# Six of 64 modulation rows move from TensorE to VectorE, in the opening and in the last attention body

## The chip, the cores and the metric

The kernel runs on one core of a Trainium2 chip. The metric is the device time of one execution in microseconds; the median of the runs counts.

## The reference, cut to what matters

Two transformer blocks run one after the other on 256 tokens of width 2048, all in float32. The first one is modulated by a vector `c`:

```python
c_act = jax.nn.silu(c)
mod = c_act @ ada_w[l] + ada_b[l]                    # ada_w: 2048 x (6 * 2048)
sh1, sc1, g1, sh2, sc2, g2 = jnp.split(mod, N_MOD, axis=-1)
h = rms_norm(x, mix_pre_g[l]) * (1.0 + sc1) + sh1
y = hybrid_mixer(h, ...)      # proj = h @ w_in; attention over q, k, v; u = a * sigmoid(g),
                              # depthwise conv with 31 taps, layer_norm, silu; mix @ w_out
x = x + g1 * rms_norm(y, mix_post_g[l])
h = rms_norm(x, ffn_pre_g[l]) * (1.0 + sc2) + sh2
x = x + g2 * rms_norm(swiglu_ffn(h, ...), ffn_post_g[l])
```

The six parts of `mod` are parts 0 to 5. Parts 0 and 1 are made first, from a tensor of their own. Part 2 (`g1`) is wanted at the end of the first mixer, part 3 (`sh2`) and part 4 (`sc2`) after it, part 5 (`g2`) after the first feed-forward.

## The kernel before, in words

**Products.** Every weight arrives from HBM in halves: a half is 128 partitions x 1024 floats (512 KB), one slot of a ring of four (`RING`). SyncE issues the load once VectorE has finished with the slot, ScalarE rounds it (`w_hi`, line 580), VectorE makes the rest (`w_lo`, line 1173), and TensorE multiplies it with the rounded and the remaining part of the activations: 24 matmuls with 256 columns. ScalarE and VectorE work up to three halves ahead of TensorE (`LEAD`). A half that TensorE takes in the opening is recorded at lines 2078 to 2080, one of the attention bodies and of `w_out` at lines 2205 to 2207.

**Order of the stages around the change.** First the opening: eight column groups of `w_in` (those of `a` and `g`), whose last quarter is the loop `for g in range(OPEN)`. Then four bodies of twelve halves (q, k and v of two heads each), with the attention of the heads before between them (`attend1`), and the taps of the convolution on ScalarE and VectorE (`CONV_UNITS`, `CONV_OPS`, a count for each step). In the last body comes the layer norm of the convolution: its sums are products with `ones` at line 2244. Then `w_out` with 32 halves.

**The rows.** A row is 128 rows of `ada_w` for one part, 128 x 2048 floats (1 MB); each of parts 2 to 5 has 16. Row number `a` counts on from 0 (rows 0 to 15 are part 2, 16 to 31 part 3, 32 to 47 part 4). GpSimd issues the loads in order into a ring of three slots, `ADA_SLOT[a] = a % 3` up to row 47; a load waits until the row that was in its slot before has been used (`ada_load`, line 523). A row is used in one of two ways:

- On TensorE (`ada_row`, `ada_products`, line 2018): four matmuls with the row as the moving side, recorded as eight. These are the rows in `TIMED`.
- On VectorE (`early_row`, lines 1418 and 1420): `acc` is set to the row times its entry of `cact`, or has it added. These are the rows in `SUMMED`. `sum_rows` on TensorE (line 2215) then adds `acc` over the partitions to the bank in which TensorE has its own rows of the part.

Before, part 2 has all its 16 rows on TensorE: six in the opening (one ahead of each half from g = 2) and ten in body 0 (one ahead of each of the halves n = 0 to 9). Part 3 has twelve on TensorE (two each ahead of n = 0, 4 and 9 of bodies 1 and 2) and four on VectorE (n = 3 and 7). Of part 4, rows 32 to 35 are on TensorE in body 3 (n = 5, 7, 9, 11), rows 36 and 38 in `w_out`, and the other ten on VectorE in `w_out`. ScalarE copies the finished bank (`copy_rows`), and TensorE turns it into columns (`turn_rows`).

Every engine takes its instructions in order, and every wait is on a semaphore that another engine or a transfer raises.

Of the kernel before, what the change touches and what calls it, by code (L numbers as in the profile page):

```python
# [7 lines left out]
KT = D // 128  # L8
# [37 lines left out]
ADA_HEADS = (tuple(range(10)), (0, 0, 4, 4, 9, 9), (0, 0, 4, 4, 9, 9), (5, 7, 9, 11))  # L46
ADA_HEADS_ADDED = ((), (3, 7), (3, 7), ())
# [7 lines left out]
SUMMED = [a for a in range(4 * KT) if KT < a < 2 * KT and a % 8 in (2, 5) or a == 2 * KT + 5 or a >= 2 * KT + 7]  # L55
TIMED = [a for a in range(4 * KT) if a not in SUMMED]
SUMMED_3 = sum(a < 2 * KT for a in SUMMED)
# [95 lines left out]
def build(nc, tokens, params, conv_taps, f_bias, ada_first, ada_w, w_in, w_out, w_gate, w_up, w_down, w_in_2, w_f_2,  # L153
# [4 lines left out]
    with ctx:  # L158
# [411 lines left out]
        def _(act):  # L570
# [224 lines left out]
            def heads1(pair, last=False):  # L795

                body = 0 if pair is None else pair + 1
                for n in range(12):
                    convert()
                    if last and n == 11:  # L800
                        act.activation(warm[:, :], eps[:, 0:1], ACT.Silu)
                    if pair is None and n == 10:
                        act.wait_ge(ada_used, KT)
                        copy_rows(2, B_N)
                    if last and n == 1:
                        act.wait_ge(acc_summed, 1)
# [12 lines left out]
                    if last and n == 10:  # L819
                        root(SEQ, (ln_summed, 1), DA)  # L820
# [7 lines left out]
            for n in range(32):  # L828
# [13 lines left out]
                if n == 25:  # L842
                    act.wait_ge(acc_summed, 2)
# [320 lines left out]
        def _(dve):  # L1164
# [242 lines left out]
            def early_row(first=False):  # L1407
# [7 lines left out]
                if first:  # L1415
                    if summed:
                        dve.wait_ge(acc_summed, 1)
# [36 lines left out]
            taken = 0  # L1454
            for g in range(OPEN):
# [3 lines left out]
                convert()  # L1459
                conv_ops(g)  # L1460
# [54 lines left out]
            for body in range(4):  # L1515
                for n in range(12):
# [13 lines left out]
                    if n in ADA_HEADS_ADDED[body]:  # L1530
                        early_row(summed == 0)
# [21 lines left out]
            for n in range(32):  # L1553
# [12 lines left out]
                if n in ADA_ADDED:  # L1566
                    early_row(n == ADA_ADDED[0])
# [406 lines left out]
        def _(pe):  # L1974
# [40 lines left out]
            def ada_products(rows, slot, kt, b):  # L2015

                for g in range(4):
                    mm = pe.matmul(bank[32 * g:32 * g + 32, b, :], cact[:, kt:kt + 1].to_broadcast([128, 32]),  # L2018
                                   rows[:, slot, 512 * g:512 * g + 512], start=kt == 0, stop=kt == KT - 1 and b == B_N)
                return mm  # L2020

            def ada_row(n, b):
# [4 lines left out]
                ada_products(ada_raw, slot, ADA_ROW[a][1], b).then_inc(ada_used, 1)  # L2027
# [183 lines left out]
            def sum_rows(n):  # L2211

                pe.wait_ge(row_added, n)
                for g in range(4):
                    mm = pe.matmul(bank[32 * g:32 * g + 32, 3, :], ones[:, 0:32], acc[:, 512 * g:512 * g + 512],
# [3 lines left out]
            for body in range(4):  # L2219
                v_ready = used[2]  # L2220
                for n in range(12):
# [4 lines left out]
                    if body == 0 and n == 8:  # L2226
                        pe.wait_ge(ag_up, 4)
                    if body == 1 and n == 1:
                        turn_rows(2, B_N)
                    if body == 3 and n == 0:  # L2230
                        sum_rows(SUMMED_3)
# [17 lines left out]
            for n, (j, q) in enumerate(W_OUT_ORDER):  # L2249
# [9 lines left out]
                if n == 24:  # L2259
                    sum_rows(SUMMED_4)  # L2260
# [310 lines left out]
```

## Time and profile before

| | us |
|---|---|
| median of 3 runs | 2547.87 (2547.27 to 2548.66) |
| the profiled execution | 2548.51 |
| its span | 2546.7 |
| TensorE busy | 2511.7 (99%) |
| VectorE busy | 1719.6 (68%) |
| ScalarE busy | 1282.8 (50%) |
| GpSimd busy | 61.1 (2%) |

The span runs from the first to the last instruction; the 1.8 us between it and the time lie around it. Busy time of TensorE is that of matmuls whose ends are modelled, so 99% says that it almost never waits, not that it is at its peak.

### The profile page before, as it was taken

What the parts mean: (1) busy time and instruction counts of PE and PEld (TensorE: products, weight loads), DVE (VectorE), ACT (ScalarE), POOL (GpSimd) and SP (SyncE); (2) the same over time, 40 slices, a digit from 0 to 9 for tenths busy, and PEclk for the clock granted to TensorE, in tenths of its full rate; (3) what the DMA queues carried; (4) which work ended last, traced back from release to release, by engine and by line L of the source; (5) the groups of instructions that cost most, each with busy time, mean ns of one, the idle gap of its engine ahead of it and who ended that gap; (6) DMA issues with size and microseconds to landing.
All of it is one profiled execution on the core that took longest, in us unless ns stands there. A gap on an engine that the chain in (4) does not pass through costs nothing.

```text
span 2546.7 us, 53371 instructions
## 1 busy us (share of the span) xinstructions
PE 2511.7 (99%) x21196; PEld 2435.4 (96%) x21196; DVE 1719.6 (68%) x2252; ACT 1282.8 (50%) x1827; POOL 61.1 (2%) x120
## 2 busy tenths in 40 slices
PE   7999999999999999999999999999999999999999
PEld 5778889999999999999999999999999999999999
DVE  5778977866666666558656655554866666677667
ACT  3378765644444444446545544444644444444445
POOL 0010000000000000000100000000000000000000
PEclk8999999999999999999999999999999999999999
DMA  9998778476666666565555555555455555555554
GB/s 399 395 403 340 289 254 303 157 231 224 225 223 228 229 224 192 182 196 157 181 164 165 160 186 180 188 182 184 146 185 193 179 189 196 185 187 187 185 182 141
DMA packets 136609, 547.36 MB, mean 215 GB/s; under 512 B 15312, under 2 KB 15568, under 8 KB 124080
## 3 DMA queue, kind: packets, MB, share of 16 engines
q1 hardware_dynamic: 126288, 474.08, 56.0%
q0 software_dynamic: 9760, 68.94, 7.2%
q10 hardware_dynamic: 448, 2.75, 0.3%
q8 instruction: 81, 1.33, 0.2%
q14 instruction: 32, 0.26, 0.0%
HBM read 543.59 MB, written 2.12 MB: 214 GB/s over the span
## 4 chain that ended last, share of the span: by engine, by line
PE 94%; DVE 2%; DMA 2%; ACT 2%; issue 0%; SPq 0%; DVEq 0%; ACTq 0%
PE bank L1994 20%; PE bank L1996 20%; PE bank L1995 20%; PE bank L2205 9%; PE bank L2207 8%; PE bank L2206 8%; DMA ada_pre<-in_ada_first 2%; PE bank L2018 1%; PE bank L2078 1%; PE bank L2080 1%; PE bank L2079 1%; PE bank L2145 1%; DMA raw<-in_w_in 1%; DVE w_lo L1173 1%; ACT w_hi L580 1%; PE bank L2163 0%
## 5 line engine op out<-in xcount | busy, mean ns | idle before, releaser
L1173 DVE TENSOR_TENSOR w_lo<-raw,w_hi 128x1024 fp32r<-128x1024 f32 x836 | 1014.0, 1223 | 620.6 <-ACT w_hi L580 619.0
L580 ACT ACTIVATE w_hi<-raw 128x1024 fp32r<-128x1024 f32 x836 | 874.5, 1057 | 783.9 <-PE bank L1996 447.4
L1994 PE MATMUL bank<-h_hi,w_hi 128*128 128x258 f32 (+1 forms) x2576 | 730.8, 284 | 2.0 <-DVE h_lo L1259 0.8
L1995 PE MATMUL bank<-h_lo,w_hi 128*128 128x258 f32 (+1 forms) x2576 | 727.2, 282 | 0.0
L1996 PE MATMUL bank<-h_hi,w_lo 128*128 128x258 f32 (+1 forms) x2576 | 727.1, 282 | 0.0
L1994 PEld LDWEIGHTS bank<-h_hi,w_hi 128*128 128x128 f32 x2576 | 485.1, 188 | 5.6 <-issue 3.0
L1995 PEld LDWEIGHTS bank<-h_lo,w_hi 128*128 128x128 f32 x2576 | 485.1, 188 | 0.6 <-issue 0.5
L1996 PEld LDWEIGHTS bank<-h_hi,w_lo 128*128 128x128 f32 x2576 | 485.1, 188 | 0.0
L2205 PE MATMUL bank<-hid_hi,w_hi 128*128 128x256 f32 x1280 | 353.9, 277 | 0.0
L2206 PE MATMUL bank<-hid_lo,w_hi 128*128 128x256 f32 x1280 | 353.7, 276 | 0.0
L2207 PE MATMUL bank<-hid_hi,w_lo 128*128 128x256 f32 x1280 | 353.7, 276 | 0.0
L1994 PE MATMUL bank<-h_whole_hi,w_hi 128*128 128x256 f32 x1280 | 353.6, 276 | 0.0
L1996 PE MATMUL bank<-h_whole_hi,w_lo 128*128 128x256 f32 x1280 | 353.4, 276 | 0.0
L1995 PE MATMUL bank<-h_whole_lo,w_hi 128*128 128x256 f32 x1280 | 353.4, 276 | 0.0
L2205 PEld LDWEIGHTS bank<-hid_hi,w_hi 128*128 128x128 f32 x1280 | 240.3, 188 | 1.7 <-issue 1.7
L1994 PEld LDWEIGHTS bank<-h_whole_hi,w_hi 128*128 128x128 f32 x1280 | 240.3, 188 | 1.7 <-DVE tu L1597 0.8
L2207 PEld LDWEIGHTS bank<-hid_hi,w_lo 128*128 128x128 f32 x1280 | 240.5, 188 | 0.0
L2206 PEld LDWEIGHTS bank<-hid_lo,w_hi 128*128 128x128 f32 x1280 | 240.3, 188 | 0.0
L1995 PEld LDWEIGHTS bank<-h_whole_lo,w_hi 128*128 128x128 f32 x1280 | 240.3, 188 | 0.0
L1996 PEld LDWEIGHTS bank<-h_whole_hi,w_lo 128*128 128x128 f32 x1280 | 240.2, 188 | 0.0
L1618 DVE TENSOR_TENSOR y<-y,bank 128x512 f32<-128x512 f32 x176 | 120.5, 685 | 47.2 <-PE bank L2207 47.0
L2205 PE MATMUL bank<-h_hi,w_hi 128*128 128x256 f32 x384 | 110.0, 286 | 0.0
(280 smaller groups left out, 3484.5 us busy)
## 6 DMA issues: line engine op xcount, KB each, us to landing
raw<-in_w_in SPq DMA_DIRECT2D x208, 512.0 KB, 4.2
raw<-in_w_ffn_up SPq DMA_DIRECT2D x176, 512.0 KB, 4.2
ada_raw<-in_ada_w POOLq DMA_DIRECT2D x64, 1024.0 KB, 8.3
raw<-in_w_gate SPq DMA_DIRECT2D x88, 512.0 KB, 4.3
raw<-in_w_up SPq DMA_DIRECT2D x88, 512.0 KB, 4.2
raw<-in_w_down SPq DMA_DIRECT2D x88, 512.0 KB, 4.2
raw<-in_w_ffn_down SPq DMA_DIRECT2D x88, 512.0 KB, 4.4
ada_pre<-in_ada_first SPq DMA_DIRECT2D x32, 1024.0 KB, 11.2
```

Source lines behind the costliest of these rows:

```text
L580: act.activation(w_hi[:, slot], raw[:, slot], ACT.Copy).then_inc(hi_ready, 1)
L1173: dve.tensor_tensor(w_lo[:, slot], raw[:, slot], fp(w_hi[:, slot]), ALU.subtract).then_inc(lo_ready, 1)
L1618: dve.tensor_tensor(y[:, 2 * j:2 * j + 2, SB], y[:, 2 * j:2 * j + 2, SB], both(b), ALU.add)\
L1994: pe.matmul(dst, wh, x_hi(kt), start=first and k == 0, stop=False)
L1995: pe.matmul(dst, wh, x_lo(kt), start=False, stop=False)
L1996: mm = pe.matmul(dst, wl, x_hi(kt), start=False, stop=last and k == len(kts) - 1)
L2018: mm = pe.matmul(bank[32 * g:32 * g + 32, b, :], cact[:, kt:kt + 1].to_broadcast([128, 32]), rows[:, slot, 512 * g:512 * g + 512], start=k ...
L2078: pe.matmul(dst, wh, h1_hi[:, kt, :], start=first, stop=False, skip_group_check=True)
L2079: pe.matmul(dst, wh, h1_lo[:, kt, :], start=False, stop=False, skip_group_check=True)
L2205: pe.matmul(dst, wh, x_hi(kt), start=first and k == 0 and o == 0, stop=False, skip_group_check=True)
L2206: pe.matmul(dst, wh, x_lo(kt), start=False, stop=False, skip_group_check=True)
L2207: mm = pe.matmul(dst, wl, x_hi(kt), start=False, stop=end, skip_group_check=True)
```

## The change

- **Part 2.** Rows 0, 1, 2 and 4 go from TensorE to VectorE: two before the loop over g, one each after the conversion of g = 1 and g = 3. TensorE begins its rows at g = 3 with row 3 (then 5, 6, 7, 8), and has seven in body 0 (n = 0 to 6). A new `sum_rows` at n = 8 of body 0 adds `acc` to the bank of part 2.
- **Part 3.** The same rows as before on either engine. TensorE's pairs that stood ahead of n = 0 of bodies 1 and 2 now stand at n = 1, behind the scores of `attend1`.
- **Part 4.** Rows 34 and 35 go from TensorE (n = 9 and 11 of body 3) to VectorE (n = 8 and 10, between steps of the layer norm). So the first row on VectorE in `w_out` is an addition and no longer a first product.
- **Convolution.** Steps of `CONV_OPS` and `CONV_UNITS` are shifted among body 0 and the first steps of body 1; the totals stay.

```diff
-ADA_HEADS = (tuple(range(10)), (0, 0, 4, 4, 9, 9), (0, 0, 4, 4, 9, 9), (5, 7, 9, 11))
-ADA_HEADS_ADDED = ((), (3, 7), (3, 7), ())
+ADA_HEADS = (tuple(range(7)), (4, 4, 9, 9), (4, 4, 9, 9), (5, 7))
+ADA_HEADS_ADDED = ((), (3, 7), (3, 7), (8, 10))
...
-SUMMED = [a for a in range(4 * KT) if KT < a < 2 * KT and a % 8 in (2, 5) or a == 2 * KT + 5 or a >= 2 * KT + 7]
+SUMMED = [a for a in range(4 * KT) if a in (0, 1, 2, 4) or KT < a < 2 * KT and a % 8 in (2, 5) or 2 * KT + 1 < a < 2 * KT + 4 or a == 2 * KT + 5 or a >= 2 * KT + 7]
...
-CONV_OPS = (0, 0, 0, 0, 1, 2, 3, 3, 3, 3, 4, 3, 3, 3, 4, 3, 3, 3, 2, 2, 3, 2, 1, 3, 2, 0, 2, 3,
+CONV_OPS = (0, 0, 0, 0, 1, 3, 3, 3, 3, 3, 4, 3, 3, 3, 3, 3, 2, 2, 2, 2, 4, 2, 2, 3, 2, 0, 2, 3,
...
-CONV_UNITS = (0, 0, 0, 0, 2, 1, 1, 1, 1, 1, 1, 2, 1, 1, 2, 1, 1, 2, 0, 2, 0, 1, 1, 0, 0, 2, 1, 1,
+CONV_UNITS = (0, 0, 0, 0, 2, 1, 1, 1, 1, 2, 1, 1, 2, 1, 1, 1, 1, 1, 1, 1, 1, 1, 1, 0, 0, 2, 1, 1,
...
                     if pair is None and n == 10:
-                        act.wait_ge(ada_used, KT)
+                        act.wait_ge(acc_summed, 1)
                         copy_rows(2, B_N)
...
             taken = 0
+            early_row(True)
+            early_row()
             for g in range(OPEN):
                 dve.wait_ge(half_used, done.next())
                 if g % 2:
                     gated(OPEN_BANK[g], g // 2)
                 convert()
+                if g in (1, 3):
+                    early_row()
                 conv_ops(g)
...
             for g in range(OPEN):
-                if g == 2:
+                if g == 3:
                     pe.wait_ge(ag_sig, 1)
-                if g >= 2:
+                if g >= 3:
                     ada_row(ada, B_N)
                     ada += 1
                 opened(g, 3)
...
+                    if body == 0 and n == 8:
+                        sum_rows(SUMMED_2, B_N)
...
                     if body:
                         attend1(n, v_ready)
+                    if body in (1, 2) and n == 1:
+                        for _ in range(2):
+                            ada_row(ada, 3)
+                            ada += 1
```

## Rows read from the trace of the kernel before

**Rows 1.** The page: busy time, share of the span and instructions of TensorE

```profile
PE 2511.7 (99%) x21196; PEld 2435.4 (96%) x21196; DVE 1719.6 (68%) x2252; ACT 1282.8 (50%) x1827; POOL 61.1 (2%) x120
```

**Rows 2.** Busy time by stretch, then granted clock, DMA share, GB/s

```profile
136.00:160.00 24.00, 24.00 (x198) 18.20 (x197) 11.41 (x13) 15.77 (x27) 3.17 (x6) 1.00 1.00 400
```

**Rows 3.** DMA queues, 150 to 196 us: what all of them moved

```profile
DMA packets 3534, 19.13 MB, mean 416 GB/s; under 512 B 393, under 2 KB 393, under 8 KB 2010
```

**Rows 4.** Timeline of TensorE: start us, us, line, operation

```profile
141.09 1.06 PE L2018 MATMUL bank<-ada_raw,cact 128*32 128x512 f32 x8
...
145.03 1.06 PE L2018 MATMUL bank<-ada_raw,cact 128*32 128x512 f32 x8
...
199.95 0.28 PE L2205 MATMUL bank<-h_hi,w_hi 128*128 128x256 f32 x1
...
202.67 0.28 PE L2205 MATMUL bank<-h_hi,w_hi 128*128 128x256 f32 x1
```

**Rows 5.** Timeline of TensorE: halves before and after a sum

```profile
410.93 0.28 PE L2205 MATMUL bank<-c_hi,w_hi 128*128 128x256 f32 x1
...
413.75 1.06 PE L2215 MATMUL bank<-acc,ones 128*32 128x512 f32 x8
...
417.58 0.28 PE L2205 MATMUL bank<-a_hi,w_hi 128*128 128x256 f32 x1
```

**Rows 6.** Timeline of VectorE: conversions, with idle time before them

```profile
128.78 3.43 DVE L1173 TENSOR_TENSOR w_lo<-raw,w_hi 128x1024 fp32r<-128x1024 f32 x3
138.09 1.23 DVE L1173 TENSOR_TENSOR w_lo<-raw,w_hi 128x1024 fp32r<-128x1024 f32 x1 [5.89 <-ACT w_hi L580]
...
140.60 1.23 DVE L1173 TENSOR_TENSOR w_lo<-raw,w_hi 128x1024 fp32r<-128x1024 f32 x1 [0.68 <-ACT w_hi L580]
```

**Rows 7.** Rows on VectorE: min/median/max ns of first products and additions

```profile
L1418 DVE TENSOR_SCALAR acc<-ada_raw,cact x2: 1277/1279/1281, 222.4 to 368.5; 128x2048 f32<-128x2048 f32 x2
L1420 DVE SCALAR_TENSOR_TENSOR acc<-ada_raw,cact,acc x12: 2342/2345/2351, 236.8 to 411.2; 128x2048 f32<-128x2048 f32 x12
```

**Rows 8.** Timeline of GpSimd: issues of rows 0, 1 and 2

```profile
126.44 1.77 POOL L523 DMA_DIRECT2D ada_raw<-in_ada_w  x3 [122.22 <-DVE mod L1298]
```

**Rows 9.** Issue to landing, us (last): rows 0, 1, 2 and row 3

```profile
ada_raw<-in_ada_w POOLq DMA_DIRECT2D x1, 1024.0 KB, 5.5
...
ada_raw<-in_ada_w POOLq DMA_DIRECT2D x1, 1024.0 KB, 8.3
...
ada_raw<-in_ada_w POOLq DMA_DIRECT2D x1, 1024.0 KB, 11.5
...
ada_raw<-in_ada_w POOLq DMA_DIRECT2D x1, 1024.0 KB, 8.7
```

**Rows 10.** Issue to landing of all 64 rows

```profile
DMA to landing us min/median/max: 5.0/8.3/13.0
```

**Rows 11.** Busy time by stretch at the start, granted clock third from last

```profile
14.00:18.00 4.00, 0.42 (x4) 0.00 (x0) 0.80 (x2) 1.00 (x2) 0.00 (x0) 1.00 1.03 422
18.00:22.00 4.00, 3.89 (x14) 2.12 (x15) 3.31 (x4) 2.96 (x4) 0.00 (x0) 0.57 1.01 418
```

**Rows 12.** Timelines of body 3 and w_out: TensorE, VectorE

```profile
333.86 1.13 PE L2244 MATMUL bank<-ln_sum,ones 128*128 128x256 f32 x4 [0.70 <-DVE ln_sum L1512]
...
350.84 0.28 PE L2205 MATMUL bank<-c_hi,w_hi 128*128 128x256 f32 x1
...
348.86 1.43 DVE L1564 TENSOR_TENSOR c_lo<-cv,c_hi 128x256 fp32r<-128x256 f32 x4
```

**Rows 13.** Body 2: first pair, load of row 28, its landing, next pair

```profile
249.56 1.92 PE L2018 MATMUL bank<-ada_raw,cact 128*32 128x512 f32 x16
...
251.81 0.53 POOL L523 DMA_DIRECT2D ada_raw<-in_ada_w  x1 [0.33 <-PE bank L2018]
...
ada_raw<-in_ada_w POOLq DMA_DIRECT2D x1, 1024.0 KB, 13.0
...
263.79 2.15 PE L2018 MATMUL bank<-ada_raw,cact 128*32 128x512 f32 x16
```

More of the change, by code:

```diff
@@ L54 @@
 ADA_ADDED = (7, 8, 10, 12, 14, 16, 18, 19, 20, 21)
-SUMMED = [a for a in range(4 * KT) if KT < a < 2 * KT and a % 8 in (2, 5) or a == 2 * KT + 5 or a >= 2 * KT + 7]
+SUMMED = [a for a in range(4 * KT) if a in (0, 1, 2, 4) or KT < a < 2 * KT and a % 8 in (2, 5) or 2 * KT + 1 < a < 2 * KT + 4 or a == 2 * KT + 5 or a >= 2 * KT + 7]
 TIMED = [a for a in range(4 * KT) if a not in SUMMED]
+FIRST = [min(a for a in TIMED if a // KT == part) for part in range(3)]
+SUMMED_2 = sum(a < KT for a in SUMMED)
 SUMMED_3 = sum(a < 2 * KT for a in SUMMED)
@@ L802, in heads1 @@
                     if pair is None and n == 10:
-                        act.wait_ge(ada_used, KT)
+                        act.wait_ge(acc_summed, 1)
                         copy_rows(2, B_N)
                     if last and n == 1:
-                        act.wait_ge(acc_summed, 1)
+                        act.wait_ge(acc_summed, 2)
                         copy_rows(3, 3)
@@ L842, in _ @@
                 if n == 25:
-                    act.wait_ge(acc_summed, 2)
+                    act.wait_ge(acc_summed, 3)
                     act.wait_ge(mod_ready, 1)
@@ L1415, in early_row @@
                 if first:
-                    if summed:
-                        dve.wait_ge(acc_summed, 1)
+                    if a >= KT:
+                        dve.wait_ge(acc_summed, a // KT)
                     op = dve.tensor_scalar(acc[:, :], ada_raw[:, slot], cact[:, kt:kt + 1], None, ALU.mult)
@@ L1530, in _ @@
                     if n in ADA_HEADS_ADDED[body]:
-                        early_row(summed == 0)
+                        early_row(summed in (SUMMED_2, SUMMED_3))
                     conv_ops(OPEN + 12 * body + n)
@@ L1566, in _ @@
                 if n in ADA_ADDED:
-                    early_row(n == ADA_ADDED[0])
+                    early_row(summed == SUMMED_3)
                 if n == 10:
@@ L2012, in quarter, with ada_products @@
                      range(kt0 + 4 * q, kt0 + 4 * q + 4), cols.stop - cols.start, q == 0, q == n_kt // 4 - 1)
-            def ada_products(rows, slot, kt, b):
+            def ada_products(rows, slot, kt, b, first):
                 for g in range(4):
                     mm = pe.matmul(bank[32 * g:32 * g + 32, b, :], cact[:, kt:kt + 1].to_broadcast([128, 32]),
-                                   rows[:, slot, 512 * g:512 * g + 512], start=kt == 0, stop=kt == KT - 1 and b == B_N)
+                                   rows[:, slot, 512 * g:512 * g + 512], start=first, stop=False)
                 return mm
@@ L2026, in ada_row @@
                 pe.wait_ge(ada_loaded[slot], 16 * (a // ADA_RING + 1))
-                ada_products(ada_raw, slot, ADA_ROW[a][1], b).then_inc(ada_used, 1)
+                ada_products(ada_raw, slot, ADA_ROW[a][1], b, a in FIRST).then_inc(ada_used, 1)
             def turn_rows(n, b):
@@ L2209, in half_one, with sum_rows @@
                 halves.next()
-            def sum_rows(n):
+            def sum_rows(n, b):
                 pe.wait_ge(row_added, n)
                 for g in range(4):
-                    mm = pe.matmul(bank[32 * g:32 * g + 32, 3, :], ones[:, 0:32], acc[:, 512 * g:512 * g + 512],
+                    mm = pe.matmul(bank[32 * g:32 * g + 32, b, :], ones[:, 0:32], acc[:, 512 * g:512 * g + 512],
                                    start=False, stop=True)
@@ L2230, in _ @@
                     if body == 3 and n == 0:
-                        sum_rows(SUMMED_3)
+                        sum_rows(SUMMED_3, 3)
                     if body == 3 and n == 3:
@@ L2259, in _ @@
                 if n == 24:
-                    sum_rows(SUMMED_4)
+                    sum_rows(SUMMED_4, 3)
                 if n == 27:
```

## The prediction, on record before the result was known

> **What bounds the kernel now.** I read the page first: TensorE is busy for 99% of the span [rows 1]. So any work taken from it is a gain, unless something else comes late. The second question is then what TensorE comes near to waiting for where the rows are. The stretches by stage answer it: from 136 us on TensorE is busy in all of 24.00 us, and the transfers have a share of 1.00 at 400 GB/s [rows 2]. Over the next 46 us they move 416 GB/s [rows 3]. The timelines give the rate of use: a row and a half together take 145.03 - 141.09 = 3.94 us on TensorE [rows 4] and are 1.573 MB, which asks for 399 GB/s; at 416 GB/s they arrive every 3.78 us. The opening is therefore held by TensorE with 4% to spare in the transfers. The reader is to see this: two bounds lie on top of each other, and the change moves one of them.
>
> **TensorE's work.** A half alone takes 202.67 - 199.95 = 2.72 us [rows 4], so a row costs 3.94 - 2.72 = 1.22 us; six rows fewer are -7.3 us. The new sum costs what the one at 413.75 costs: 417.58 - 410.93 = 6.65 us with two halves in it, less 5.44, is 1.21 us [rows 5]. Together -6.1 us.
>
> **VectorE's work.** The four rows of part 2 are 1.28 + 3 x 2.35 = 8.3 us, those of part 4 are 2.35 + 1.28, and the first one in w_out grows by 1.07 us [rows 7]. VectorE stands idle for 5.89 us ahead of 138.09 [rows 6], which covers the first two rows; rows 2 and 4 fall where it is busy 11.41 of 24 us [rows 2]. I cost all this at nothing. Without that cover it would be 8.3 us. The shift of convolution steps also costs nothing: the sums of both tuples are the same, and by step 1 of body 1 they are level to one operation.
>
> **The ring of three slots: where a wait appears.** Row 3 can be loaded only after row 0 has been used, row 4 after row 1, row 5 after row 2.
>
> - Row 0 is issued at 126.44 and lands 5.5 us later, at 131.9; rows 1 and 2, issued at about 127.1 and 127.7, land at 135.4 and 139.2 [rows 8, 9]. VectorE is free at 132.2 [rows 6]. It ends row 0 at 133.5, so row 3 is issued at about 133.8 (from the end of a use to the issue it takes 0.33 us: 249.56 + 1.92 = 251.48, then 251.81 [rows 13]). Row 1 ends at 137.7; row 4 is issued at 138.0.
> - Rows 1 and 2 landed 3.5 and 3.8 us apart [rows 8, 9], the rate of a full queue. Row 3 stands behind row 2: 139.2 + 3.8 = 143.0. TensorE, which came to its first row at 141.09 - 3.94 = 137.1 [rows 4] and now has none ahead of half g = 2, wants it at 137.1 + 2.8 = 139.9. **Wait 3.1 us.**
> - TensorE then ends row 3 and the next half at 143.0 + 3.9 = 146.9 and wants row 5. VectorE does row 2 only behind the conversion of g = 1, which ends at 141.8 [rows 6], so until 144.2; row 5 is issued at 144.4. At the earliest it follows row 4 (143.0 + 3.8 = 146.8) at 150.6; with the 8.7 us that row 3 took before [rows 9] it lands at 153.1. I take the middle, 151.8. **Wait 4.9 us.**
> - Row 7 needs row 4, which VectorE does at g = 3, after the half that ends at 146.9: gate, conversion and row until about 151.6. It lands at 159 to 160.6, TensorE wants it at 151.8 + 2 x 3.94 = 159.7. **Wait 0.4 us.** From there rows are used every 3.94 us and can come every 3.78: no further wait.
>
> Behind these waits stand TensorE's own halves; ScalarE and VectorE are three halves ahead and stop too. The sum is 8.4 us. The bounds: all 64 rows took 5.0 us at least [rows 10], so row 5 lands at 149.4 or later, against a TensorE that without the first wait wants it at 143.8: 5.6 us at least. At most, with 8.7 us for row 3 too, the table gives 3.1 + 6.2 + 0.9 = 10.2 us.
>
> The Trainium skill (DMA: Bandwidth & Descriptors, Anatomy of one DMA) puts a transfer from GpSimd at some 2.0 us plus its bytes at 436 GB/s, an estimate of 4.4 us for a row. By that rule row 3 would be there in time and row 5 at 148.8; the sum of the waits would be 5.0 us. The trace does not agree in this stage: no row took under 5.0 us, and row 3 took 8.7 us [rows 9, 10].
>
> **The clock.** When TensorE had worked 0.42 us in a stretch of 4, its granted clock in the next four was 0.57, against 1.00 before [rows 11]: of the two levels it was mostly at 1.2 GHz. (0.43 x 4) / 0.5 gives 3.4 us at the lower level, which costs half of that, 1.7 us. The wait of 4.9 us is longer than that idle stretch, the one of 3.1 us is shorter, and a slow half between the two waits only shortens the second. I take it once: +1.7 us (0 to 3.4). The Trainium skill (TensorE: Matmul & The Clock Gate, HAM oscillation) says the same of kernels that wait for transfers between groups of matmuls.
>
> **The pairs in bodies 1 and 2.** Moving a pair from ahead of n = 0 to n = 1 costs no work, but its slots come free a half and the scores later: about 3.5 us. In body 2 the second load behind the pair was issued at 251.81, took 13.0 us and landed at 264.8, when the next pair was already being used: the one at 263.79 lasted 2.15 us, 0.23 more than the one at 249.56 [rows 13]. There is no margin. Three and a half us later, with halves that are then further along, I put its wait at 2.0 us (0 to 3.5). Part of it is given back, because ScalarE and VectorE, who are late in the rest of this body, catch up: net +1.0 us. In body 1 I count nothing (0 to 1.0), since the trace shows no such wait there.
>
> **Body 3.** Of the two rows taken out, 2.4 us, the first is lost. At n = 10 TensorE already waits 0.70 us for the fold of the squares [rows 12], and that chain (conversion, squares, fold) hangs on half n = 7, which does not move. The row at n = 11 is gained, 1.2 us. Then n = 3 of w_out waits for `c_lo`, ready at 350.29 against 350.84 [rows 12]; the chain before it hangs on the fold, so 0.6 us can be gained there, and some 0.8 later, when the next waits are passed. I count +1.6 us given back (0 to 1.8). VectorE's rows at n = 8 and 10 lie where it waits for ScalarE's conversion, which waits for TensorE.
>
> **Sum.** -6.1 + 8.4 + 1.7 + 1.0 + 1.6 = +6.6 us. Against the profiled execution: 2548.51 + 6.6 = 2555.1; it lies 0.64 us above the median, so the forecast is 2554.5 us, 0.26% more. A change within 0.2%, 5.1 us, can hardly be told from none.
>
> **Rivals.**
>
> - *The waits come, but the clock holds and body 2 has its rows in time.* -6.1 + 8.4 + 1.6 = +3.9: 2551.8, no change by the bound. For it: the idle stretch of 3.1 us is short, and 13.0 us was the worst of 64 landings. Against it: a wait of 4.9 us.
> - *Rows land as fast as the quickest one.* At 5.0 us each [rows 10], the waits are 5.6: with body 3 the sum is +1.1, 2549.0. It decides where row 5 lands before 150. Against it: the queue is full with rows 3 and 4. The skill's formula would give about +0.5, 2548.4.
> - *TensorE never waits for a row.* Then -6.1 and, with the loss in body 3, -4.5: 2541.8 to 2543.4, faster in the first case. It needs row 5 by 143.8, before VectorE has even used row 2 (144.2) if the conversion of g = 1 is where it was. It could only be if the half it waits for lands over 5 us sooner.
> - *VectorE becomes the bound.* From 160 us on it has little idle time; if the rows delay the conversions there by their whole length, +8.3 more: about 2560. For it: every conversion stands behind them. Against it: they lie ahead of that stretch, and TensorE is standing still.
>
> **Chances and range.** Forecast 0.55, of which 0.50 slower by over 0.2% and 0.05 within; first rival 0.21, of which 0.08 over the bound, since 10.2 us of waits alone would lift it there; quick landings 0.13, within; no wait 0.07, faster; VectorE 0.04, slower. So faster 0.07, same 0.05 + 0.13 + 0.13 = 0.31, slower 0.50 + 0.08 + 0.04 = 0.62. The range goes from 2548.0 (quick landings) to 2560.0 (10.2 us of waits, clock twice, body 2 in full, less what is given back).
>
> **What would show it.** In the trace after: TensorE idle ahead of line 2018 at about 140 and 147 us, ended by a landing of `ada_raw`; issues of rows 3, 4 and 5 at 133.8, 138.0 and 144.4; a granted clock under 1.00 between 140 and 160; the last half of body 0 later than 202.67 [rows 4]; a longer wait at line 2244. The prediction is wrong if row 3 is there at 140, or if VectorE uses row 2 well before 142.

## The result, and the profile after

| | before | after |
|---|---|---|
| median of nine runs, us | 2549.63 (2547.27 to 2550.61) | 2558.47 (2555.81 to 2566.27) |
| the profiled execution, us | 2548.51 | 2555.81 |
| its span, us | 2546.7 | 2554.0 |

The ratio is 1.0038, with a 95% interval of 1.0028 to 1.0047: the change costs 0.38%, some 8.8 us by the medians and 7.3 us by the two profiled executions. Those are near the quick end of their runs: the four quickest runs after the change had a mean granted clock of 0.994 or 0.995, the other five one of 0.991 to 0.994.

**Where the loss appears.** To place it, I measure marks from the issue of row 0: the first matmul of part 2's `turn_rows`, and part 4's sum. Before, they come 210.16 - 126.44 = 83.72 us and 413.75 - 126.44 = 287.31 us behind it; after, 89.29 and 295.05 us. The first mark stands behind one pair of rows before and ahead of it after; a pair takes some 2.07 us, so like for like it is 91.36. The opening and body 0 have lost 7.64 us, and behind part 4's sum nothing changes any more (2132.9 and 2132.8 us to the span's end).

The page after, busy time by engine (TensorE with its weight loads, VectorE, ScalarE, GpSimd), answers to [rows 1]:

```profile
PE 2506.6 (98%) x21156; PEld 2433.6 (95%) x21156; DVE 1731.7 (68%) x2258; ACT 1282.9 (50%) x1827; POOL 60.3 (2%) x120
```

TensorE is busy for 5.1 us less and the kernel takes longer, so TensorE waits. Stretches of the opening after (PE, PEld, DVE, ACT, POOL busy, then granted clock, DMA share, GB/s), which answer to [rows 2]:

```profile
136.00:140.00 4.00, 3.73 (x32) 3.53 (x30) 3.76 (x3) 1.06 (x1) 0.53 (x1) 1.00 1.01 419
140.00:144.00 4.00, 0.61 (x4) 0.23 (x8) 1.95 (x2) 1.54 (x2) 0.00 (x0) 0.87 1.01 416
144.00:149.00 5.00, 4.78 (x32) 3.32 (x24) 2.96 (x3) 1.25 (x2) 1.05 (x2) 0.77 1.03 410
149.00:153.00 4.00, 0.00 (x0) 0.00 (x0) 3.60 (x3) 0.87 (x1) 0.00 (x0) 1.00 1.00 414
153.00:158.00 5.00, 4.80 (x27) 3.14 (x28) 0.39 (x1) 0.00 (x0) 1.05 (x2) 0.66 1.00 406
```

Before, TensorE was busy in all of these 22 us. Now it stands still twice, the transfers run at 406 to 419 GB/s the whole time, and around the end of each standstill the granted clock falls under 1.00. The timeline of TensorE after, at those two places:

```profile
143.39 1.94 PE L2024 MATMUL bank<-ada_raw,cact 128*32 128x512 f32 x8 [3.66 <-DMA ada_raw<-in_ada_w]
...
153.20 1.94 PE L2024 MATMUL bank<-ada_raw,cact 128*32 128x512 f32 x8 [4.43 <-DMA ada_raw<-in_ada_w]
```

Rows 3 and 5 are what it waits for, 3.66 and 4.43 us, and each row then takes 1.94 us in place of 1.06 [rows 4]. GpSimd's issues after, which answer to [rows 8], with rows 0 to 2, 3, 4, and 5 with 6:

```profile
126.12 1.77 POOL L525 DMA_DIRECT2D ada_raw<-in_ada_w  x3 [121.89 <-DVE mod L1300]
133.86 0.53 POOL L525 DMA_DIRECT2D ada_raw<-in_ada_w  x1 [5.97 <-DVE acc L1420]
138.23 0.53 POOL L525 DMA_DIRECT2D ada_raw<-in_ada_w  x1 [3.84 <-DVE acc L1422]
145.84 1.05 POOL L525 DMA_DIRECT2D ada_raw<-in_ada_w  x2 [7.08 <-DVE acc L1422]
```

Issue to landing (last column, us) after, of row 3 and of row 5, which answers to [rows 9]:

```profile
ada_raw<-in_ada_w POOLq DMA_DIRECT2D x1, 1024.0 KB, 9.4
...
ada_raw<-in_ada_w POOLq DMA_DIRECT2D x1, 1024.0 KB, 7.3
```

VectorE after: row 0, the conversion of g = 1 and row 2 (answers to [rows 6]):

```profile
132.28 1.29 DVE L1420 TENSOR_SCALAR acc<-ada_raw,cact 128x2048 f32<-128x2048 f32 x1 [0.39 <-DMA ada_raw<-in_ada_w]
...
142.06 1.23 DVE L1175 TENSOR_TENSOR w_lo<-raw,w_hi 128x1024 fp32r<-128x1024 f32 x1 [2.08 <-ACT w_hi L582]
143.20 2.35 DVE L1422 SCALAR_TENSOR_TENSOR acc<-ada_raw,cact,acc 128x2048 f32<-128x2048 f32 x1
```

The conversion at 142.06 stood at 140.60 before [rows 6]. It is late although VectorE was idle ahead of it: its half landed at 140.89 against 139.43. The queues show why. From 131 to 142 us before (queue q0 has the rows, q1 the halves: packets, MB, share):

```profile
q0 software_dynamic: 334, 2.37, 54.1%
q1 hardware_dynamic: 572, 2.09, 46.7%
```

and after:

```profile
q0 software_dynamic: 409, 2.97, 64.3%
q1 hardware_dynamic: 441, 1.63, 36.2%
```

Rows 3 and 4 are issued 4.7 and 4.3 us sooner than before. They take 0.60 MB more in these 11 us, and the halves get 0.46 MB less. The total rate hardly moves (406 and 419 GB/s). Then bodies 1 to 3, timeline of TensorE after, with the waits that were not there or shorter before:

```profile
228.91 1.06 PE L2024 MATMUL bank<-ada_raw,cact 128*32 128x512 f32 x8 [0.36 <-DMA ada_raw<-in_ada_w]
...
273.28 1.06 PE L2024 MATMUL bank<-ada_raw,cact 128*32 128x512 f32 x8 [0.97 <-DMA ada_raw<-in_ada_w]
...
342.25 0.92 PE L2256 MATMUL bank<-ln_sum,ones 128*128 128x256 f32 x3 [1.90 <-DVE ln_sum L1518]
```

**The account**, in us from the issue of row 0: opening and body 0 -3.67 (four rows at 1.22, less the new sum of 1.21), +8.09 waits, +3.4 for two stretches of 3.41 us each at half of the clock's full rate (of which some lies beside other waits); that is +7.8, measured +7.64. That leaves +0.1 up to part 4's sum: body 3 -1.0 (kernel 1 below has it alone), and so bodies 1 and 2 +1.1. Together +7.74, the difference of the two marks at part 4's sum.

### The profile page after: what moved, and what is told of

The parts are those of the page before. It is cut to its first block, busy times and chain, and to the rows that moved or that the text cites. A ratio compares the mean times of both kernels' runs of the same rounds, so it can differ in the third digit from the quotient of the medians.

```text
span 2554.0 us, 53303 instructions
## 1 busy us (share of the span) xinstructions
PE 2506.6 (98%) x21156; PEld 2433.6 (95%) x21156; DVE 1731.7 (68%) x2258; ACT 1282.9 (50%) x1827; POOL 60.3 (2%) x120
## 4 chain that ended last, share of the span: by engine, by line
PE 91%; DMA 4%; DVE 3%; ACT 1%; issue 1%; SPq 0%; DVEq 0%; ACTq 0%
PE bank L2000 20%; PE bank L2002 20%; PE bank L2001 20%; PE bank L2211 8%; PE bank L2213 8%; PE bank L2212 8%; DMA ada_pre<-in_ada_first 2%; DMA ada_raw<-in_ada_w 1%; DMA raw<-in_w_in 1%; PE bank L2024 1%; DVE w_lo L1175 1%; PE bank L2151 1%; ACT w_hi L582 1%; DVE ada_pre L1300 1%; PE bank L2169 0%
```

## The experiments

The theory: rows 3 and 5 are wanted before they can have landed, so what TensorE saves turns into waits, and each long wait costs a stretch of slow clock besides. It has two halves that can be told apart: the rows are issued late (the order in the ring), or the transfers are full (the rate). The rivals: VectorE's added work is the bound; part 4's rows or the moved pairs make the loss.

All the runs in one table. Waits are TensorE's idle times over 0.3 us from 137 to 163 us, added up; slow is the length of the stretches under full clock that begin there; the marks are those of above, with 2.07 us added to part 2's where the pairs stand behind it.

| kernel | waits | slow | turn of part 2 | sum of part 4 | median, us | ratio to before |
|---|---|---|---|---|---|---|
| before | 0 | 0 | 83.72 | 287.31 | 2549.01 to 2549.86 in the groups of runs | 1 |
| after | 8.09 | 6.8 | 91.36 | 295.05 | 2558.47 | 1.0038 [1.0028, 1.0047] |
| 1: part 4 alone, rows 34, 35 | 0 | 0 | 83.72 | 286.29 | 2550.11 | 1.0007 [0.9998, 1.0016] |
| 2: part 4 alone, rows 33, 35 | 0 | 0 | 83.72 | 284.93 | 2548.35 | 0.9996 [0.9987, 1.0005] |
| 12: part 2 alone | 9.03 | 6.8 | 91.85 | 296.82 | 2559.13 | 1.0039 [1.0026, 1.0053] |
| 3: after, pairs back ahead of n = 0 | 8.32 | 10.2 | 92.48 | 296.60 | 2558.58 | 1.0038 [1.0025, 1.0052] |
| 4: after, clock held | 2.73, and 7.2 filled | 0 | 90.18 | 293.89 | 2556.58 | 1.0034 [1.0021, 1.0046] |
| 5: after, fourth buffer | 5.40 | 3.4 | 87.76 | 291.50 | 2554.22 | 1.0021 [1.0012, 1.0031] |
| 6: after, half loads | 6.46 | 3.4 | 88.23 | 293.12 | 2554.68 | 1.0025 [1.0016, 1.0035] |
| 7: rows from half 6 | 3.68 | 0 | 84.41 | 287.93 | 2551.38 | 1.0012 [1.0003, 1.0021] |
| 8: as 7, rows 33, 35 | 2.46 | 0 | 83.61 | 286.09 | 2549.84 | 1.0002 [0.9993, 1.0012] |
| 9: as 7, half loads | 0.38 | 0 | 81.01 | 285.25 | 2548.34 | 0.9997 [0.9988, 1.0006] |
| 10: half 4, fourth buffer, rows 33, 35 | 4.54 | 6.8 | 87.57 | 290.02 | 2551.14 | 1.0004 [0.9995, 1.0013] |
| 11: as 8, fourth buffer, pairs back | 4.17 | 3.4 | 86.94 | 288.59 | 2548.18 | 0.9994 [0.9985, 1.0003] |

The reader can hold the first three columns of numbers against each other: 83.72 - 3.67 + waits + half of the slow time gives the turn of part 2 within 1.1 us in every kernel with the new part 2 (for 7: 83.73 against 84.41; for 9: 80.43 against 81.01; for 10: 88.0 against 87.57; for 4 the added matmuls count as waits). The waits and the clock are thus the opening's loss of 7.64 us, to within those 1.1 us. Each row of marks is one execution: kernels 7 and 8 run the same program up to the turn, and their marks there differ by 0.8 us.

### 1, 2 and 12: one part alone

```diff
 # 1: the kernel before, with
-ADA_HEADS = (tuple(range(10)), (0, 0, 4, 4, 9, 9), (0, 0, 4, 4, 9, 9), (5, 7, 9, 11))
-ADA_HEADS_ADDED = ((), (3, 7), (3, 7), ())
+ADA_HEADS = (tuple(range(10)), (0, 0, 4, 4, 9, 9), (0, 0, 4, 4, 9, 9), (5, 7))
+ADA_HEADS_ADDED = ((), (3, 7), (3, 7), (8, 10))
 # and rows 34 and 35 in SUMMED; 2: the same with (5, 9) and rows 33 and 35
...
 # 12: the changed kernel, with rows 34 and 35 out of SUMMED, and
-ADA_HEADS = (tuple(range(7)), (4, 4, 9, 9), (4, 4, 9, 9), (5, 7))
-ADA_HEADS_ADDED = ((), (3, 7), (3, 7), (8, 10))
+ADA_HEADS = (tuple(range(7)), (4, 4, 9, 9), (4, 4, 9, 9), (5, 7, 9, 11))
+ADA_HEADS_ADDED = ((), (3, 7), (3, 7), ())
```

Kernel 1 was expected so:

> The kernel before with only the two rows of part 4 moved (n = 9 and 11 of body 3 on TensorE, to n = 8 and 10 on VectorE). Theory (the time is lost in the opening, at rows that land late): a gain of about 1.0 us, since the row at n = 9 only lengthens the wait at line 2244 (from 0.70 to about 1.9 us) and the one at n = 11 is gained. Rival (the rows on VectorE between the steps of the layer norm cost the time): 2 us slower or more. Third possibility: both rows gained, 2.4 us faster.

Kernel 2:

> As the run with part 4 alone, but VectorE takes rows 33 and 35 and TensorE keeps row 34: TensorE's rows of body 3 stand at n = 5 and 9 in place of 5 and 7. Theory: the chain that the wait at line 2244 hangs on starts behind half n = 7, so a row taken out ahead of that half is gained in full, and the row kept at n = 9 lies in the wait: about 2.0 us faster than before, 1 us better than with rows 34 and 35, with a wait at line 2244 of about 0.7 us. Rival (TensorE's work alone counts, it does not matter where it stands): the same as with rows 34 and 35.

Kernel 12:

> Part 2 alone: the changed kernel with part 4 as before (rows 34 and 35 of part 4 on TensorE again, heads 5, 7, 9, 11 in body 3). If the parts add up, the loss is all of part 2's: waits of 3.5 to 4.5 us for rows 3 and 5, the mark of part 2's turn at 88.5 to 89.5 us behind the first issue (89.29 in the changed kernel), that of part 4's sum 1.0 us later than in the changed kernel (295.05), near 296, and the time 2557 to 2560.5 us, 1.003 to 1.0045 of before. The rival is that part 4's rows share in the loss (VectorE fuller, or the pairs and heads disturbed): then this is quicker than the changed kernel, 2555 us or less.

Timeline of TensorE ahead of the second sums of the layer norm, in kernel 1:

```profile
333.77 1.13 PE L2244 MATMUL bank<-ln_sum,ones 128*128 128x256 f32 x4 [1.90 <-DVE ln_sum L1512]
```

and in kernel 2:

```profile
333.59 1.13 PE L2244 MATMUL bank<-ln_sum,ones 128*128 128x256 f32 x4 [0.71 <-DVE ln_sum L1512]
```

Before, this wait was 0.70 us [rows 12]. Without the row at n = 9 it is 1.90: the 1.2 us saved there are stood out. With that row kept and the one at n = 7 taken out in its place, the wait stays at 0.71, and the mark of part 4's sum comes 2.4 us sooner than before in place of 1.0. Timeline of TensorE in kernel 12, rows 3 and 5:

```profile
143.69 1.94 PE L2024 MATMUL bank<-ada_raw,cact 128*32 128x512 f32 x8 [4.68 <-DMA ada_raw<-in_ada_w]
...
153.51 1.79 PE L2024 MATMUL bank<-ada_raw,cact 128*32 128x512 f32 x8 [4.35 <-DMA ada_raw<-in_ada_w]
```

Part 2 has the whole loss (1.0039), and part 4 alone has none that can be measured. The rival that part 4's rows share in the loss falls. Kernel 12 keeps the moved pairs and the shifted steps of the convolution. Kernel 3 takes the pairs back; no run takes the steps alone, and what they can cost in the opening and body 0 lies within the 1.1 us that the account leaves. The wait for row 3 is 4.68 us here against 3.66 although the row landed only 0.3 us later (143.56). TensorE's records end 0.7 us sooner in this trace; some may be missing, and the mark is only 0.5 us later.

### 3: the pairs back ahead of n = 0

```diff
-ADA_HEADS = (tuple(range(7)), (4, 4, 9, 9), (4, 4, 9, 9), (5, 7))
+ADA_HEADS = (tuple(range(7)), (0, 0, 4, 4, 9, 9), (0, 0, 4, 4, 9, 9), (5, 7))
...
-                    if body in (1, 2) and n == 1:
-                        for _ in range(2):
-                            ada_row(ada, 3)
-                            ada += 1
```

> The changed kernel with TensorE's pairs of part 3 back ahead of n = 0 of bodies 1 and 2. Theory: the waits of 0.36 and 0.97 us for rows at n = 4 of bodies 1 and 2 go, about 1.2 us faster than the changed kernel in the profile, some 6 us slower than before; the two waits in the opening stay at 3.7 and 4.4 us. Rival (the moved pairs help the attention and their move is the gain of the change): slower than the changed kernel by 1 us or more.

The waits at n = 4 of bodies 1 and 2 (0.36 and 0.97 us) went, as expected. The rest was a miss: the mark of part 4's sum comes 1.55 us later than in the changed kernel and not 1.2 sooner, and the medians are level. Up to that mark this execution had two more slow stretches of clock, one in the opening and one at 343 us. The second began behind this wait (timeline of TensorE):

```profile
342.19 1.49 PE L2252 MATMUL bank<-ln_sum,ones 128*128 128x256 f32 x4 [1.91 <-DVE ln_sum L1518]
```

The changed kernel has the same wait, of 1.90 us, with no slow stretch behind it. So the place of the pairs costs about what its two waits show, and neither the mark nor the time can resolve it.

### 4: the clock held through the waits

```diff
             for g in range(OPEN):
...
+                if g in (3, 4):
+                    pe.wait_ge(ag_up, 1)
+                    for _ in range(4):
+                        pe.matmul(bank[:, B_S, :], ident[:, :], pcol[:, 3:7, :].rearrange("p a n -> p (a n)"),
+                                  start=True, stop=True)
                 if g >= 3:
                     ada_row(ada, B_N)
```

> The changed kernel with four more matmuls of 512 columns on TensorE ahead of row 3 and again ahead of row 5, into a bank that nothing reads then, so that TensorE works while it would wait. Theory: the granted clock stays at 1.00 between 140 and 160 us (0.87, 0.77 and 0.66 in stretches of it without them). Each of the two stretches at the lower level cost about 1.6 us, but the first only shortens the wait for row 5, so about 1.5 to 2 us faster than the changed kernel, 5 to 7 us slower than before, and a smaller spread of the runs than 2555.8 to 2566.3. Rival (the clock does not matter, TensorE waits for rows anyway): no change against the changed kernel or slightly slower.

Timeline of TensorE, added matmuls and rows (the span's first issue is 1.3 us later in this execution):

```profile
140.87 3.60 PE L2144 MATMUL bank<-pcol,ident 128*128 128x512 f32 x8
144.73 1.06 PE L2024 MATMUL bank<-ada_raw,cact 128*32 128x512 f32 x8 [0.26 <-DMA ada_raw<-in_ada_w]
148.57 3.59 PE L2144 MATMUL bank<-pcol,ident 128*128 128x512 f32 x8
154.89 1.06 PE L2024 MATMUL bank<-ada_raw,cact 128*32 128x512 f32 x8 [2.73 <-DMA ada_raw<-in_ada_w]
```

The clock stays at 1.00 throughout the opening, and the row takes 1.06 us again, not 1.94. The sum of part 4 comes 1.2 us sooner, and the median is 1.9 us lower. That is less than the 3.4 us of the account, because the time is partly handed over: without the slow half between them, the second standstill is 3.59 + 2.73 = 6.3 us and not 4.43. Row 5 landed at 154.84, which is 0.4 us later from the issue of row 0 on than in the changed kernel. The landing sets the end, not TensorE. The six runs lie closer together too (2555.85 to 2559.1, clock 0.995 or 0.996).

### 5: a fourth buffer for the rows of part 2

```diff
-ADA_SLOT = [a % 3 for a in range(3 * KT)] + [a % 2 for a in range(KT)]
+ADA_SLOT = [a % 4 for a in range(KT)] + [a % 3 for a in range(KT, 3 * KT)] + [a % 2 for a in range(KT)]
...
+        ada_more = place("ada_more", "r2", 8384, [128, D])
```

> This is the changed kernel with a fourth ada_raw buffer for the rows of part 2 alone, so that row 3 is issued straight behind row 2 and each later row waits for the use of the row four before it. Everything else is as in the changed kernel, where TensorE waits 3.66 us for row 3 (landed 143.26) and 4.43 us for row 5 (landed 153.16). If the waits come from when the rows are issued (the order: a buffer that comes free late), both go nearly altogether: row 3 is issued near 128 and row 5 behind row 1's sum near 138, the opening takes 8 us less and the 3.2 us of low clock go too, so the mark of part 4's sum comes some 10 us sooner, near 284 us behind the first issue against 295. If they come from how fast the transfers move beside the halves' own loads (the rows before 3 took 4.3 to 6.6 us each to follow each other at 132.25, 135.56, 139.31, 143.26), row 3 still lands near 142 to 143 and waits 2.5 to 3.7 us, and row 5 lands a row earlier than now, near 149 to 151, with 2 to 4 us of wait. I expect the second: a gain of 1 to 4 us on the time, 2554 to 2557 us.

The landings that the expectation names lie 3.3, 3.8 and 4.0 us apart, not 4.3 to 6.6. Issue to landing of row 3, issued at 127.68 (the second line is the buffer `ada_more`):

```profile
ada_raw<-in_ada_w POOLq DMA_DIRECT2D x1, 1024.0 KB, 10.9
ada_more<-in_ada_w POOLq DMA_DIRECT2D x1, 1024.0 KB, 15.3
```

Timeline of TensorE, rows 3 and 5:

```profile
143.10 1.57 PE L2031 MATMUL bank<-ada_more,cact 128*32 128x512 f32 x8 [3.54 <-DMA ada_more<-in_ada_w]
...
150.56 1.06 PE L2031 MATMUL bank<-ada_raw,cact 128*32 128x512 f32 x8 [1.86 <-DMA ada_raw<-in_ada_w]
```

Row 3 is issued 6.2 us sooner and lands 0.3 us sooner, at 142.96: its wait is the rate's alone. Row 5 is issued 8.9 us sooner and lands 2.65 us sooner, at 150.51, one row's time behind the row ahead of it: of its wait, 2.6 us were the ring's.

### 6: half of the bytes for rows 3 to 15

This kernel leaves out half of the data of rows 3 to 15; so does kernel 9.

```diff
-                gp.dma_start(ada_raw[:, slot], ada_w[128 * kt:128 * kt + 128, (part - 2) * D:(part - 1) * D])\
+                w = D // 2 if 3 <= a < KT else D
+                gp.dma_start(ada_raw[:, slot, 0:w], ada_w[128 * kt:128 * kt + 128, (part - 2) * D:(part - 2) * D + w])\
```

> The changed kernel with the loads of rows 3 to 15 cut to half of their columns, so that half of those rows' data is left out (the products and the waits stay as they are, over what the buffer holds). The issues keep their order and their waits for buffers, and each of those transfers moves half. If the rate of the transfers sets the two waits, row 3 lands some 2 to 3 us sooner (near 140 to 141) and row 5 too, and each wait falls to 0 to 2 us. If the buffer's late release sets them, row 3's issue at 133.86 and row 5's at 145.84 stay, a landing takes perhaps 4 us in place of 7.3 to 9.4, and row 5's wait, counted from its issue, is still 1 to 2 us, row 3's none. Both act in the changed kernel by my account, so I expect row 3's wait near 0 to 1 and row 5's near 1 to 2, and the time 5 to 9 us under the changed kernel's, 2550 to 2554 us.

Timeline of TensorE, rows 3, 5 and 7:

```profile
142.45 1.94 PE L2025 MATMUL bank<-ada_raw,cact 128*32 128x512 f32 x8 [2.63 <-ACT sigg L719]
149.64 1.06 PE L2025 MATMUL bank<-ada_raw,cact 128*32 128x512 f32 x8 [1.82 <-DMA ada_raw<-in_ada_w]
159.58 1.06 PE L2025 MATMUL bank<-ada_raw,cact 128*32 128x512 f32 x8 [2.01 <-DMA ada_raw<-in_ada_w]
```

The name in the first bracket misleads: the sigmoid that TensorE waits for ended at 134.8, and the second one, which it does not wait for, happened to end at 142.33, beside the row's landing at 142.31. Row 5's wait came out as expected. Row 3 was a miss: it landed 0.95 us sooner and not 2 to 3; the rows ahead of it in the queue are whole. The median, 2554.68, lies just above the expected 2550 to 2554. Row 7 has a new wait of 2.01 us: its slot comes free only when VectorE has used row 4, at 152.4, behind the conversion of g = 3. So in this kernel the order still costs.

### 7, 8 and 9: TensorE's rows from half 6

```diff
-ADA_HEADS = (tuple(range(7)), (4, 4, 9, 9), (4, 4, 9, 9), (5, 7))
+ADA_HEADS = (tuple(range(10)), (4, 4, 9, 9), (4, 4, 9, 9), (5, 7))
...
-                if g >= 3:
+                if g >= 6:
                     ada_row(ada, B_N)
...
-                    if body == 0 and n == 8:
+                    if body == 0 and n == 10:
                         sum_rows(SUMMED_2, B_N)
```

Kernel 8 has rows 33 and 35 of kernel 2 besides, kernel 9 the loads of kernel 6. Kernel 7:

> The changed kernel, but TensorE's rows of part 2 begin at half 6 of the opening in place of half 3: two rows in the opening and ten in body 0, with part 2's sum at n = 10. The same twelve rows on TensorE and four on VectorE. If the loss of the change is that rows 3 and 5 are asked for before they can have landed, both waits (8.1 us) and the two stretches at 1.2 GHz behind them (3.2 us) go: the halves 3 to 5 go by without a row, and the only waits left are those of halves whose own loads share the queues, 1 to 3 us. The mark of part 2's turn comes at 79 to 82 us behind the first issue (89.29 in the changed kernel, 83.72 before), that of part 4's sum at 285 to 288 (295.05 and 287.31), and the time is 2545 to 2549 us, same as before or faster. If the loss is the work itself or VectorE's added rows (VectorE as the bound), the time stays near 2558 us.

Kernel 8:

> As the kernel whose rows of part 2 begin at half 6, and of part 4 VectorE takes rows 33 and 35 in place of 34 and 35, TensorE keeping row 34 at n = 9. With the kernel before as its base that placing came 1.4 us sooner than rows 34 and 35 at the mark of part 4's sum (284.93 against 286.29). If the two add up, this ends 1 to 1.5 us under the half-6 kernel, near 2544 to 2547 us, under both the kernel before and the changed one; if the wait ahead of body 3's sums is set by VectorE's later rows, now that everything comes sooner, the gain is nothing.

Kernel 9:

> The half-6 kernel (TensorE's rows of part 2 begin at half 6) with the loads of rows 3 to 15 cut to half of their columns, so that half of those rows' data is left out; products and waits stay. The half-6 kernel still waits 3.68 us in the opening (1.59 and 0.78 us for two halves' own loads, 0.67 and 0.64 us for two rows) and its part 2 turns only 1.4 us sooner behind the first issue than before, though TensorE has four rows less there. If what is left is the rate of the transfers (both kernels run at 410 to 430 GB/s there), the four waits fall to under 1.5 us in all, and the mark of part 2's turn comes at 79.5 to 80.5 us in place of 82.34. If it is the order (the buffers and the steps that issue), the waits stay near 3.5 us and the mark near 82. I expect the first, with the time 2 to 3 us under the half-6 kernel's 2551.4.

Timeline of TensorE in kernel 7, its waits in the opening and the first steps of body 0:

```profile
145.54 0.39 PE L2084 MATMUL bank<-h_hi,w_hi 128*128 128x256 f32 x1 [1.59 <-DVE w_lo L1175]
149.32 0.39 PE L2084 MATMUL bank<-h_hi,w_hi 128*128 128x256 f32 x1 [0.78 <-DVE w_lo L1175]
156.92 1.06 PE L2024 MATMUL bank<-ada_raw,cact 128*32 128x512 f32 x8 [0.67 <-DMA ada_raw<-in_ada_w]
161.65 1.06 PE L2024 MATMUL bank<-ada_raw,cact 128*32 128x512 f32 x8 [0.64 <-DMA ada_raw<-in_ada_w]
```

The same work on both engines as in the changed kernel, in another order, is 7.1 us quicker by the medians: VectorE as the bound falls. It was idle ahead of the conversion that ended the first of these waits (timeline of VectorE):

```profile
144.26 1.22 DVE L1175 TENSOR_TENSOR w_lo<-raw,w_hi 128x1024 fp32r<-128x1024 f32 x1 [2.79 <-ACT w_hi L582]
```

But it is still no quicker than before. I had expected 2545 to 2549 us, and the median of 2551.38 is 0.12% over the kernel before, by an interval that leaves out 1. Where no row stands ahead of the halves, TensorE comes to two of them 0.9 and 1.7 us after they land (143.09 and 146.85), before they are converted. With 3.68 us of waits against 3.67 us of work saved, nothing is gained. Kernel 9 shows that these waits are the rate's; its only one in the opening, and its 24 us from 136 on:

```profile
156.46 1.06 PE L2025 MATMUL bank<-ada_raw,cact 128*32 128x512 f32 x8 [0.38 <-DMA ada_raw<-in_ada_w]
```

```profile
136.00:160.00 24.00, 23.62 (x198) 20.67 (x197) 19.90 (x21) 18.36 (x32) 3.16 (x6) 1.00 0.93 345
```

With fewer bytes wanted (345 GB/s, against 383 in kernel 7) the saved work shows at last: the turn comes 2.7 us sooner than before (78.94 us as it stands, a little under the expected band). Kernel 8 adds 33 and 35 to kernel 7 and comes 1.8 us sooner at the mark of part 4's sum. Of that, 0.8 us were there at the turn of part 2, where the two programs are still the same; 1.0 us came behind it, where kernel 2 gained 1.4 over kernel 1. Its median of 2549.84 is above what I expected (2544 to 2547); its runs lie between 2544.17 and 2552.6.

### 10 and 11: the fourth buffer with a later start

Kernel 10 is 5 with `g >= 4`, one more row in body 0, the sum at n = 9, and rows 33 and 35. Kernel 11 is 8 with the fourth buffer, the pairs back ahead of n = 0, and part 2's sum at n = 11.

> The changed kernel with three edits at once: the fourth buffer for part 2's rows, TensorE's rows from half 4 in place of half 3 (four in the opening, eight in body 0, the sum at n = 9), and rows 33 and 35 in place of 34 and 35 on VectorE. With the fourth buffer alone row 3 landed at 142.96 and was asked for at 139.5, row 5 at 150.51, asked for at 148.65; a half later both are asked for 3.9 us later, by when they have landed, so the two waits go, but the halves' own loads (landed near 143 and 145) may cost 1 to 2 us. Mark of part 2's turn 81 to 83, of part 4's sum 284.5 to 286.5 (before 287.31, half 6 with rows 33 and 35 286.09), time 2546 to 2549 us. If the rate of the transfers sets everything, the mark of the turn stays at 82 or over whatever the order, and the time is no better than the 2549.8 of half 6 with rows 33 and 35.

> As the kernel of half 6 with rows 33 and 35, with the fourth buffer and with the pairs of bodies 1 and 2 ahead of n = 0 again, as in the kernel before. The buffer brings rows' issues forward and the pairs are asked for 3.9 us sooner, so the wait of 0.8 us at n = 4 of body 2 should go and nothing else wait for it, if the pair's rows have landed by n = 0, as they had before and with the pairs back in the changed kernel. The fourth buffer adds no bytes: if rate sets the opening's waits (0.59, 0.79 and 1.08 us), they stay. I expect the mark of part 4's sum at 285 to 286.5 and the time 2547.5 to 2550 us; it would beat the kernel before by 2 us or more only if the opening's waits went, which I do not expect.

Timeline of TensorE in kernel 10, rows 3 and 5:

```profile
143.63 1.06 PE L2031 MATMUL bank<-ada_more,cact 128*32 128x512 f32 x8 [1.02 <-DMA ada_more<-in_ada_w]
151.15 1.94 PE L2031 MATMUL bank<-ada_raw,cact 128*32 128x512 f32 x8 [3.52 <-DMA ada_raw<-in_ada_w]
```

Kernel 10 refuted my forecast for it (a mark of 81 to 83; it was 87.57 like for like, 85.5 as it stands). The wait for row 3 was 2.5 us shorter than in kernel 5, and no slow stretch came behind it. So TensorE wanted row 5 1.1 us sooner (147.63 against 148.70), and it landed 0.6 us later (151.10 against 150.51): that wait grew by 1.7 us. A wait moved from one row to the next. That is what a stage does whose pace the transfers set, and the condition for it had been put beside the forecast. In kernel 11 the pair's wait at n = 4 went, but the opening's did not stay as expected: they grew from 2.46 us in kernel 8 to 4.17, for halves now, of which the last was for one that landed at 159.88, and a slow stretch came behind it. The mark of part 4's sum, 288.59, missed the expected 285 to 286.5. The median of 2548.18 lies in the expected band all the same; the profiled execution, 2550.55, was the slowest of the eleven. With kernel 2's median it is the lowest of any whole kernel here, but neither can be told from the kernel before. No version was found that beats it by more than the measurement's uncertainty.

## Why the prediction came out as it did

The forecast was 2554.5 us in a range of 2548.0 to 2560.0, slower by over 0.2%, with 0.62. The median is 2558.47, slower by 0.38%. The mechanism was right; the size was 4.0 us short. Of that, 1.8 us are the median of the kernel before, which went from 2547.87 over three runs to 2549.63 over nine. Between the profiled executions it was +7.3 against +6.6. By its steps:

- **TensorE's work, -6.1.** Borne out for part 2: with the waits and the clock added back, -3.67 closes the account of eleven kernels within 1.1 us. TensorE's busy time fell by 5.1 us in spite of the slow stretches.
- **VectorE's work at nothing.** Shown by kernel 7. VectorE's busy time grew by 12.1 us, and the predicted sum was 13.0.
- **Row 3's wait, 3.1.** It was 3.66: TensorE wanted the row at 139.73 (forecast 139.9), it landed at 143.26 (143.0) and its first product began at 143.39. Kernel 5 shows that the argument was the right one: behind row 2 in a full queue, whatever the issue.
- **Row 5's wait, 4.9.** It was 4.43, but two terms of it were off and cancelled. It landed at 153.16, the late bound of the forecast and not the middle of 151.8: row 2 was used 1.4 us later than forecast (143.20 to 145.55), because the conversion of g = 1 was itself pushed back by the rows' earlier loads, which the prediction left where it was. And TensorE wanted it at 148.78, not 146.9, because the slow stretch behind the first wait came on top. That the wait came within 0.5 us of the forecast is luck.
- **Row 7's wait, 0.4.** None.
- **The clock, once, +1.7.** This is the step that failed most in size. The wait of 3.66 us brought a slow stretch too, so there were two of 3.41 us. They cost 3.4 us in the account. Kernel 4 gets 1.2 us of it back by the mark and 1.9 by the median. The Trainium skill (TensorE: Matmul & The Clock Gate, HAM oscillation) tells of kernels whose clock falls at each wait for a transfer between groups of matmuls; the trace agrees for the two long waits, and not for that of 0.97 us at 273 us, behind which the row took 1.06 us. All eight waits of 3.5 us and more that these traces show from 60 us on had a slow stretch that began within them or at most 1.2 us behind them. Shorter ones did not decide it: behind the wait of 1.9 us at the layer norm's sums it came in kernels 3 and 6, and in the kernels after, 1, 4, 5, 7 and 9 it did not.
- **The pairs of bodies 1 and 2, +1.0.** By the account +1.1, but composed otherwise: waits of 0.36 and 0.97 us where 0 and 2.0 were forecast, and nothing given back.
- **Body 3, +1.6 given back.** Measured: a gain of 1.0 us where the prediction had 0.8 (2.4 less 1.6). Kernel 1 shows the wait of 1.90 us that eats the row at n = 9, and kernel 2 that another row pays twice as much.
- **The rivals.** That the clock holds fell. That rows land at 5.0 us each fell: row 3 took 9.4 and row 5 took 7.3. That TensorE never waits, and that VectorE is the bound, fell too.

What the prediction saw in its first paragraph, 4% to spare in the transfers, was worth more than it made of it. It is why part 2 gained in no order tried: kernel 7 has, from the issue of row 0 on, neither of the long waits nor their slow stretches, and is still no better than before. Not settled is the rest of the difference between medians and profiled executions. It goes with the granted clock of the runs (0.991 to 0.995 after), of which only the profiled ones have a trace that shows where it fell. Kernel 3 shows that one execution can have a slow stretch where another, with the same wait, has none.

## What to carry to other kernels

Before work is taken off the busiest engine in a stage, compare the rate at which it wants its data with the rate at which the data comes: with 4% between them, 3.7 us of saved work in the opening and body 0 came back as 3.7 us of waiting even with the rows asked for later. When the users of one ring are split between two engines, work out when each element can land, and start the second engine's share so late that it never asks sooner; the same work with its rows three halves later took 7 us less. Where an engine, once a piece of work is taken from it, only waits longer for another engine (the row ahead of n = 9), take the work from another place (the row ahead of n = 7).

## What the runs showed of the hardware

- **Where both have work waiting, two queues share the engines by packets, not by bytes.** With whole rows, q0 and q1 had 148 and 156 packets from 136 to 140 us in the changed kernel, and q0 moved nearly twice the bytes:

```profile
DMA packets 305, 1.68 MB, mean 419 GB/s; under 512 B 31, under 2 KB 31, under 8 KB 172
...
q0 software_dynamic: 148, 1.08, 64.7%
q1 hardware_dynamic: 156, 0.58, 35.2%
```

  In kernel 9, where from row 3 on a row's packet is half as long:

```profile
DMA packets 391, 1.64 MB, mean 411 GB/s; under 512 B 37, under 2 KB 37, under 8 KB 346
...
q0 software_dynamic: 188, 0.86, 52.4%
q1 hardware_dynamic: 202, 0.76, 46.9%
```

  The packets are level again, and the bytes come near to it. Where one queue runs dry the count is another: in the kernel before no packet of a row starts from 138.65 to 140.89 us (row 3 is issued at 138.55), and from 138 to 142 the two queues had 43 and 344. So the queue with the longer packets takes the larger share, and a row issued early delays the halves beside it: in kernel 10 the half issued at 131.96 us took 17.2 us to land, and the same half in the kernel before, issued at 132.23, took 10.8. The Trainium skill (Trainium Kernel Development and Optimization, Key Constraints) says that transfers from all issuing engines run on the same sixteen and interleave; these rows agree, and give the share in which they do.
- **The one core that runs drew 417 GB/s over 70 us on end** (kernel 5, 130 to 200 us; 410 in the kernel before). The Trainium skill (HBM Reference, Specifications (TRN2)) gives about 425 GB/s for a core that streams alone; the trace agrees nearly, with 416 [rows 3].
- **A name in a bracket can be a coincidence.** In kernel 6 a wait for a row that landed at 142.31 us was put down to a sigmoid that ended at 142.33; the program waits there only for an earlier one, which ended at 134.8.
